# A two-block transformer kernel in which 96 instead of 64 tokens take the gathered expert path, 416 instead of 448 stay dense, and VectorE instead of GpSimd writes the low parts of the expert weights from the 53rd column on

## What is computed

```python
def peer_ffn(x, w_q, sub_keys, expert_u, expert_v):
    ...
    e = (jnp.take_along_axis(i1, ci // P_TOPK, axis=-1) * N_KEYS
         + jnp.take_along_axis(i2, ci % P_TOPK, axis=-1))
    g = jax.nn.softmax(vals, axis=-1)
    ...
        a = jnp.einsum('cd,ckd->ck', xc, expert_u[ec])
        w = (gc * jax.nn.gelu(a.astype(jnp.float32))).astype(x.dtype)
        return jnp.einsum('ck,ckd->cd', w, expert_v[ec])
```

## Time and profile before

| | us |
|---|---|
| median of three runs (lowest, highest) | 2789.0 (2784.4, 2793.2) |
| profiled execution, span | 2786.5 |
| TensorE busy | 2673.9 |
| VectorE busy | 1865.4 |
| GpSimd busy | 1708.2 |
| ScalarE busy | 907.8 |

### The profile page before, as it was taken

One profiled execution on the slowest core, in us unless ns is written; L12 is line 12 of the kernel. 1 busy time (PEld: TensorE's weight loads), 2 busy tenths in 40 slices (PEclk: granted clock), 3 DMA queues, 4 the chain that ended last, 5 costly groups with the idle time before them and its releaser, 6 DMA issues.

```text
span 2786.5 us, 36945 instructions
## 1 busy us (share of the span) xinstructions
PE 2673.9 (96%) x13184; PEld 2229.0 (80%) x13184; DVE 1865.4 (67%) x2466; ACT 907.8 (33%) x1531; POOL 1708.2 (61%) x755
## 2 busy tenths in 40 slices
PE   6999999999997999998999999999999999999999
PEld 4777778888874876445888888999998999999998
DVE  7999973372335525764549983999964677777777
ACT  2223222101123144663234343444432333333332
POOL 5888887878873611003745555777786566666665
PEclk9999999999998998999999999999999999999999
DMA  3443334423331321001325555888898676767764
GB/s 143 134 135 131 129 124 137 134 95 133 114 109 59 113 99 68 1 1 63 114 98 151 142 150 176 259 286 286 286 325 314 238 263 240 270 248 260 259 248 162
DMA packets 171121, 466.67 MB, mean 167 GB/s; under 512 B 12832, under 2 KB 86688, under 8 KB 171040
## 3 DMA queue, kind: packets, MB, share of 16 engines
q1 hardware_dynamic: 152608, 398.53, 43.2%
q0 software_dynamic: 18432, 67.12, 6.7%
HBM read 404.78 MB, written 60.82 MB: 167 GB/s over the span
## 4 chain that ended last, share of the span: by engine, by line
PE 80%; issue 7%; DVE 6%; POOL 4%; ACT 1%; DMA 1%; POOLq 0%; SPq 0%; DVEq 0%; ACTq 0%
PE ps L1016 37%; PE ps L553 30%; POOL spl L2091 3%; PE ps L951 2%; PE ps L1037 2%; PE ps L644 1%; PE ps L928 1%; PE ps L911 1%; PE ps L569 1%; DVE hnt L1490 1%; DVE hl L1494 1%; PE ps L907 1%; PE ps L870 1%; PE ps L739 1%; PE ps L816 1%
## 5 line engine op out<-in xcount | busy, mean ns | idle before, releaser
L2091 POOL TENSOR_TENSOR spl<-ring,spl 128x1024 fp32r<-128x1024 f32 x256 | 669.9, 2617 | 482.6 <-ACT spl L1368 482.4
L2024 POOL TENSOR_TENSOR spl<-ring,zero 128x1024 fp32r<-128x1024 f32 (+1 forms) x180 | 367.7, 2043 | 528.2 <-PE ps L553 459.9
L553 PE MATMUL ps<-hh,spl 128*128 128x512 f32 x2064 | 652.3, 395 | 20.3 <-DVE hl L1494 7.9
L1016 PE MATMUL ps<-wsp,spl 128*128 128x448 f32 x3072 | 626.7, 366 | 4.6 <-issue 4.6
L1016 PEld LDWEIGHTS ps<-wsp,spl 128*128 128x128 f32 x3072 | 578.3, 188 | 50.6 <-POOL spl L2091 5.0
L1016 PE MATMUL ps<-hh,spl 128*128 128x448 f32 x2048 | 601.4, 369 | 6.7 <-POOL spl L2091 6.7
L1368 ACT ACTIVATE spl<-ring 128x1024 fp32r<-128x1024 f32 x256 | 271.7, 1061 | 795.4 <-PE ps L1016 793.8
L2026 POOL TENSOR_TENSOR spl<-ring,spl 128x1024 fp32r<-128x1024 f32 (+1 forms) x180 | 479.5, 2664 | 14.1
L553 PEld LDWEIGHTS ps<-hh,spl 128*128 128x128 f32 x2064 | 389.9, 189 | 115.5 <-issue 15.4
L1982 DVE TENSOR_TENSOR wsp<-gl,wsp 128x448 fp32r<-128x448 f32 x128 | 315.3, 2464 | 167.6 <-ACT wsp L1413 167.3
L1016 PEld LDWEIGHTS ps<-hh,spl 128*128 128x128 f32 x2048 | 385.3, 188 | 42.4 <-issue 9.3
(11 more groups left out here) (341 smaller groups left out, 3291.1 us busy)
## 6 DMA issues: line engine op xcount, KB each, us to landing
ring<-stream_in SPq DMA_DIRECT2D x196, 704.0 KB, 4.1
ring<-u_in SPq DMA_DIRECT2D x128, 512.0 KB, 4.1
ring<-v_in SPq DMA_DIRECT2D x128, 512.0 KB, 3.5
gelu<-gst SPq DMA_DIRECT2D x128, 224.0 KB, 4.1
dense<-stage SPq DMA_DIRECT2D x14, 2048.0 KB, 13.9
gl<-gelu SPq DMA_DIRECT2D x32, 896.0 KB, 5.8
gw<-dense SPq DMA_DIRECT2D x32, 896.0 KB, 8.5
x<-x_in SPq DMA_DIRECT2D x4, 512.0 KB, 6.8
```

The costliest lines, as they stand in the source:

```text
L553: m = pe.matmul(ps[:, bank, :], w[:, part, k0 + k * n:k0 + k * n + P], rhs(k), start=first and k == 0 and part == 0 and rhs is high, stop= ...
L1016: m = pe.matmul(ps[:, bank, 0:TD], w[:, part, k0 + k * P:k0 + (k + 1) * P], rhs(k), start=first and k == 0 and part == 0 and rhs is high, ...
L2024: pool.tensor_tensor(w[:, 0, 0:n], ring[:, j, 0:n], zero[:, :].to_broadcast([P, n]), ALU.add).then_inc(wt_high, 1)
L2091: pool.tensor_tensor(spl[:, j % 2, 1, 0:D], ring[:, j, 0:D], spl[:, j % 2, 0, 0:D].bitcast(F32), ALU.subtract).then_inc(lo_done, 1)
```

## The change

96 tokens take the gathered path, in two blocks: the last 64 as before (two partition halves, 64 gathers), and the 32 before them four times (four partition quarters, 32 gathers), with rows, accumulator and fold matmuls of their own (`xt2`, `acc2`, `folds[1]`). 416 tokens stay dense: every dense matmul streams 416 columns, every save, gate load and `weigh` shrinks alike, and there are 13 slabs and not 14, so the one-hots, spreads and stores end four units earlier, after unit 103. The gathered rows of the v stage have six slots and not four. From unit 52 on VectorE writes the low parts (`weight_low`), placed by hand among its one-hots, dots, `low`, `weigh` and `add_row`; GpSimd then only issues gathers. 36 dots are spread in the one-hot loop (6 in 8 units, as before), two in the last slab, and the other 58 lie in the 23 units 105 to 127, two or three ahead of each unit's low part.

```diff
@@ -47,11 +47,15 @@
 GB = 16
 TB = 32
 QUAD = 4
-RARE = 64
+PICKS = E_H * E_K
+RARE_BLOCKS = [(64, 2), (32, 4)]
+RARE = sum(n for n, _ in RARE_BLOCKS)
 TD = T - RARE
 SLABS = TD // TB
-RARE_SLOTS = E_H * E_K // 2
-U_SLOTS, V_SLOTS = 6, 4
+RARE_AT = [0, PICKS // 2]
+RARE_SLOTS = sum(PICKS // k for _, k in RARE_BLOCKS)
+U_SLOTS, V_SLOTS = 6, 6
+SPREAD_DOTS = 6
...
+def rare_slot(s, i=0, per=0):
+
+    m, r = divmod(s, 3)
+    if r < 2:
+        return 0, i * (per // 3 * 2) + (RARE_AT[0] + 2 * m + r)
+    return 1, i * (per // 3) + (RARE_AT[1] + m)
...
-                        m = pe.matmul(bank[half * RARE:(half + 1) * RARE, :], rows[:, c, TD:T].bitcast(F32), cc("ident"),
+                        m = pe.matmul(bank[half * 64:(half + 1) * 64, :], rows[:, c, T - 64:T].bitcast(F32), cc("ident"),
+                                      start=rows is hh, stop=rows is hl)
+            for c in range(DC):
+                bank = ps[:, 6 + c // 4, c % 4 * P:(c % 4 + 1) * P]
+                for rows in (hh, hl):
+                    for part in range(4):
+                        m = pe.matmul(bank[part * 32:(part + 1) * 32, :], rows[:, c, TD:TD + 32].bitcast(F32), cc("ident"),
...
-                            pe.wait_ge(acc_done, RARE_SLOTS + 1)
-                        pe.matmul(ps[:, c % DC, TD:T], acc[:, c % DC * P:(c % DC + 1) * P], fold, start=True, stop=True)\
+                            pe.wait_ge(acc_done, RARE_SLOTS + 2)
+                        pe.matmul(ps[:, c % DC, TD:TD + 32], acc2[:, c % DC * P:(c % DC + 1) * P], folds[1], start=True, stop=True)
+                        pe.matmul(ps[:, c % DC, T - 64:T], acc[:, c % DC * P:(c % DC + 1) * P], folds[0], start=True, stop=True)\
                             .then_inc(y_part, 1)
...
+            def weight_low(at, i=None, per=0):
+
+                dve.wait_ge(hi_done, at + 1 if i is None else i * per + (at + 1))
+                dve.tensor_tensor(spl[:, at % 2, 1, 0:D], ring[:, at % RING, 0:D], spl[:, at % 2, 0, 0:D].bitcast(F32),
+                                  ALU.subtract).then_inc(lo_done, 1)
+
+            def dot(s, i=None):
+
+                row = s % U_SLOTS
+                dve.wait_ge(u_row[row], 16 * (s // U_SLOTS + 1) if i is None else i * 16 + 16)
+                block, at = rare_slot(s, i if i is not None else 0, SPREAD_DOTS)
+                dve.scalar_tensor_tensor(out=rows_of[row], in0=rows_of[row], scalar=1.0, in1=xts[block], op0=ALU.mult, op1=ALU.mult,
+                                         accum_out=dots[:, one_at(at)]).then_inc(dot_done, 1)
+
+            dve.wait_ge(lo_done, RING + U_PLAIN)
+            weight_low(U_PLAIN)
...
+            with dve.Fori(0, SLABS // 2) as b:
+                    one_hots(j, b, bass.ds(b * (4 * GB) + j * GB, GB))
+                    weight_low(U_PLAIN + 2 * j + 1, b, 8)
+                    for s in range(j * SPREAD_DOTS // 4, (j + 1) * SPREAD_DOTS // 4):
+                        dot(s, b)
+                    weight_low(U_PLAIN + 2 * j + 2, b, 8)
+            s, last = SLABS // 2 * SPREAD_DOTS, U_PLAIN + 4 * SLABS
+            for j in range(2):
+                at = SLABS // 2 * 4 * GB + j * GB
+                one_hots(j, SLABS // 2, slice(at, at + GB))
+                weight_low(last - 4 + 2 * j + 1)
+                dot(s)
+                s += 1
+                weight_low(last - 4 + 2 * j + 2)
+            first, left = last + 1, RARE_SLOTS - s
+            for e in range(first, N_KEYS):
+                for _ in range(left * (e - first + 1) // (N_KEYS - first) - left * (e - first) // (N_KEYS - first)):
+                    dot(s)
+                    s += 1
+                weight_low(e)
+            dve.wait_ge(oh_ready, 2 * SLABS)
...
+            def unit_pair(i, p, to_weigh=None):
+
+                for k in (2 * p, 2 * p + 1):
+                    weight_low(N_KEYS + k, i, 16)
+                    low(i, k)
+                if to_weigh is not None:
+                    weigh(*to_weigh)
+                for s in range(p * 12 // 8, (p + 1) * 12 // 8):
+                    add_row(i, s)
...
-            u_at, v_at = 0, 0
-            for n in range(U_PLAIN, 2 * N_KEYS):
-                column(n // RING, n % RING)
-                while u_at < RARE_SLOTS and u_unit_of(u_at) <= n:
-                    u_gather(u_at)
-                    u_at += 1
-                while u_at == RARE_SLOTS and v_at < RARE_SLOTS and N_KEYS + 2 * v_at - 3 <= n:
-                    v_gather(v_at)
-                    v_at += 1
+            for s in range(RARE_SLOTS):
+                u_gather(s)
+            for s in range(RARE_SLOTS):
+                v_gather(s)
```

More of the change, by code:

```diff
@@ L505, in _ @@
                             store(i, k)
+            for j in range(RING):
+                u_load(U_PLAIN // 4 + 1 + SLABS, j)
+                save_late(U_PLAIN // 4 + 1 + SLABS, j)
+                if j == 1:
+                    store(SLABS // 2, 0)
             for i in range(U_PLAIN // 4 + 2 + SLABS, N_KEYS // 4):
@@ L1072, in _ @@
                     spread(i, 2 * k + 1)
+            for k in range(4):
+                u_unit(U_PLAIN // 4 + SLABS - 1, k)
+                spread(SLABS // 2, 2 * k)
+                spread(SLABS // 2, 2 * k + 1)
             with pe.Fori(U_PLAIN // 4 + SLABS, N_KEYS // 4) as i:
@@ L1430, in _ @@
                     evacuate(i, 2 * k + 1)
+            for k in range(4):
+                gelu_unit(U_PLAIN // 4 + SLABS - 1, k)
+                evacuate(SLABS // 2, 2 * k)
+                evacuate(SLABS // 2, 2 * k + 1)
             with eng.Fori(U_PLAIN // 4 + SLABS, N_KEYS // 4 - 1) as i:
@@ L1928, in _, with late @@
-            for half in range(2):
-                dve.tensor_copy(share[half * RARE:(half + 1) * RARE, :],
-                                sel[P - RARE:, TT - 1, 2, half * RARE_SLOTS:(half + 1) * RARE_SLOTS]).then_inc(share_ready, 1)
-            step(dve.tensor_tensor(fold, cst[:, CST["ident"][0]:CST["ident"][0] + RARE],
-                                   cst[:, CST["ident"][0] + RARE:CST["ident"][1]], ALU.add))
-            def dot(s, row, ready):
-                dve.wait_ge(u_row[row], ready)
-                dve.scalar_tensor_tensor(out=u_rows[row], in0=u_rows[row], scalar=1.0, in1=xt, op0=ALU.mult, op1=ALU.mult,
-                                         accum_out=dots[:, s]).then_inc(dot_done, 1)
+            def late(block, part, k):
+                n, parts = RARE_BLOCKS[block]
+                first = TD % P + sum(m for m, _ in RARE_BLOCKS[block + 1:])
+                return sel[first:first + n, TT - 1, k, part * PICKS // parts:(part + 1) * PICKS // parts]
@@ new lines, in picks_of @@
+            def picks_of(tile, block, part):
+                n, parts = RARE_BLOCKS[block]
+                return tile[part * n:(part + 1) * n, RARE_AT[block]:RARE_AT[block] + PICKS // parts]
+            parts_of = [(block, part) for block in range(2) for part in range(RARE_BLOCKS[block][1])]
+            for block, part in parts_of:
+                dve.scalar_tensor_tensor(out=picks_of(place, block, part), in0=late(block, part, 1), scalar=float(N_KEYS),
+                                         in1=late(block, part, 0), op0=ALU.mult, op1=ALU.add).then_inc(place_ready, 1)
```

110 lines of the change are left out of this document (50 added, 60 removed).

## The result

The changed kernel takes 2706.7 us (median of 4 runs, 2701.3 to 2708.8); the kernel before took 2786.7 us beside it (4 runs, 2782.5 to 2793.2). The ratio is 0.9708, with a 95% interval of 0.9682 to 0.9733: 2.9% faster. The profiled execution took 2706.1 us with a span of 2704.2. All medians and ratios leave out slow executions, that is one, among the six of the kernel with the first low parts ahead of the gelu, at 7632 us.

What follows compares the result with a forecast made beforehand. The prediction took the number of matmuls by the distance between them, plus few waits, as the bound. Savings of 75.2 us less 24 and 6 us of new waits gave 45 us off 2786.5: 2742 us, range 2715 to 2775.

Steps and rivals of the forecast that it cites:

- rows turned: Before unit 0, more tokens turned into rows: 128 more matmul records, taken as a cost of 5.5 us.
- the new waits: TensorE waiting behind VectorE's low parts between units 105 and 130, as transfers saturate: 15 to 45 us.
- The last 23 u units and the turn: Units 105 to 127 move 49.8 MB at 359 GB/s, 24 us of waits; 6 us more at the v stage's start.
- The transfers keep up: Rival: gathers and loads run at 400 GB/s or more, waits under 12 us, time 2720 to 2728 us; chance 0.17.
- The v stage: 128 units of 24 matmuls, each 13.3 ns shorter with 416 columns: 40.9 us saved.
- Units 0 to 51: Early u units: 16.6 us saved by shorter matmuls, less grown waits for GpSimd's low parts, leaving 11.2 us.
- The first one-hots: At the first spread, TensorE's 5.5 us wait for VectorE's first one-hots falls by 2.0 us.
- the slab less: One slab fewer leaves 4 units without spreads: 3.6 us saved.
- units 52 to 104: Middle u units, with shorter matmuls and low parts hidden on VectorE: 19.9 us saved.
- VectorE's order is too tight: Rival: v stage misses its 0.5 us or spread stretch stays at 281 GB/s; 2752 to 2778 us; chance 0.17.
- gathers one at a time: Rival: in the last u units each gather must land before the next moves; about 2987 us, at least 2831; chance 0.05.
- 416 columns are no faster: Rival: another limit holds matmuls at about 200 ns, so 82 us do not come; about 2810 us; chance 0.04.

Runs made afterwards that it cites:

- mixed passes: The 448-column kernel with VectorE low parts and the changed kernel, each v-stage pass multiplying four different widths; one execution each, 2766.4 and 2691.5 us.

## Why the prediction was wrong

**The mechanism was right, a rate was wrong.** Every term of the sum but the rows turned shows with its sign, the low parts on VectorE are hidden in the spread stretch (5.51 us a unit, forecast 5.50) and in the v stage, and the new waits stood where they were put, from unit 105 on, with a share over 1.0: 11.0 us behind VectorE's low parts, and 4.1 behind ScalarE. Four sizes were off, all to the same side.

**The last 23 u units and the turn: 15.8 us of the 37.** This is the step that failed, "At 359 GB/s ... it takes 139 us". The measured rate is 411 GB/s over units 105 to 126, and 418 in the stretch inside. The row of 359 GB/s was hardly one "of loads and gathers". Its packets, from 2040 to 2050 us in the kernel before, and then those of the changed kernel from 2015 to 2110 us:

```profile
DMA packets 4562, 3.59 MB, mean 359 GB/s; under 512 B 64, under 2 KB 4227, under 8 KB 4562
```

```profile
DMA packets 12377, 39.71 MB, mean 418 GB/s; under 512 B 1375, under 2 KB 3992, under 8 KB 12375
```

93% of the packets of the first are under 2 KB, most of them of the slab's store that SyncE had issued at 2035.9 us (2 MB in pieces of 512 bytes, 128 numbers in `QUAD * TB`), and only 0.87 of its 3.59 MB are gathers. In the second it is 32%. Full stretches beside such a store moved 359, 341 and 311 GB/s (shares 1.07, 1.06 and 1.02), full ones without it 406, 411 and 418 (1.02, 1.03 and 1.03). No run changed the size of the packets alone, so that they set the rate is read from these stretches, not tested. My 49.8 MB over 418 GB/s are 119 us, 14.6 more than the 104.5 that TensorE needs; units 105 to 126 took 114.1 - 99.4 = 14.7 us more than the same units without waits. Of these 11.0 are waits and 1.6 a lower clock behind one of them. The 4 MB that I let lag would have brought it to 5.

That is 10.3 us of the 15.8; the other 5.6 are the turn. I had put 6 us there; the piece of units 127 and 128 takes 16.6 us against 16.8 before, and 14.9 when there is no backlog. The transfers are behind there, but before the change about as much was lost for another reason (4.6 us between the stages), and the two do not add up.

None of the rivals fits as written. *The transfers keep up* had the right condition (400 GB/s or more) and a chance of only 0.17. But the transfers did not keep up: the waits of 15.1 us are over its 12 and at the lower end of the forecast's own 15 to 45, and the time is under its 2720 to 2728, since the other terms were off to the same side. For the rate, a page spoke for it: the Trainium skill (DMA: Bandwidth & Descriptors, "Where 436 GB/s comes from") gives the 435 GB/s, and the 418 over 95 us come near it. The same section also says that transfers between HBM and SBUF are bound at about 358 GB/s a core. The trace does not agree: nearly all of the 411 and 418 GB/s are such transfers. Of small packets the page ("Why small descriptors are slow") says that each costs about three cycles whatever its size. That agrees in kind with the lower rate beside the slab's store. By an estimate from the page's count a piece of 512 bytes loses 3 cycles in 19, some 16%; no run here tests that figure.

**The v stage: 7.2 us.** "The bounds are 12.9 and 14.2" ns for 32 columns. In the profiled execution it was 202.7 - 186.7 = 16.0 ns (564.48 us for 126 units of 24). In five other executions with 416 columns and VectorE's low parts the same units take 569.5 to 572.3 us (the longest with 2.3 us of waits), 188.3 ns, and there it is 14.4. The matmuls from 2190 to 2620 us, without a wait, in the changed kernel and in the one with eight dots a pass:

```profile
2190.00:2620.00 430.00, 430.00 (x2306) 429.33 (x2305) 1.00 0.81 300
```

```profile
2190.00:2620.00 430.00, 430.00 (x2285) 427.45 (x2284) 1.00 0.80 298
```

The kernel with the first low parts ahead of the gelu has the faster pace too (x2305). The runs with other widths show why bounds by lines from 280 and 512 columns could not hold: the extra over the columns changes with the width, and 448 has more of it than both ends. The term was mis-sized by 3 us or by 8, depending on the pace. Only one execution of each variant was profiled, so what decides between the two stays open.

**Units 0 to 51: 7.4 us.** Of TensorE's busy time 258.3 - 238.8 = 19.5 us went, 15.6 ns a matmul instead of 13.3: 2.9 us of the miss. The rest are the waits. I let them grow by 3.9 us (each of 12 by 0.32) and 1.5 more; they grew from 6.0 to 6.9. Without the long one of 2.2 us before, which has no successor, eleven waits went from 0.35 us on average (3.8 / 11) to 0.63 (6.9 / 11), so the 0.3 us each were right. The base was not: two other executions with 448 columns and the same code in these units waited 2.4 us (ten times) and 3.2 (eleven times) over the same stretch. From there to 6.9 it is 3.7 to 4.5, near what I added, so most of this part of the miss seems to be that the profiled execution before waited longer than others do.

**Rows turned: 5.8 us.** I put 128 records at 57 ns, 7.3 us, or half of it, and took 5.5. Four column quarters do overlap more than two halves: 128 records in 3.6 us, 28 ns each. The rest is not explained by the change; the start of unit 0 differs by up to 9 us between executions.

**What held.** The first one-hots 3.8 us (3.5 forecast); the slab less and units 52 to 104 within 1 us; VectorE's low parts 1224 ns and dots 1220 ns beside GpSimd's gathers; no waits in the v stage, where by my estimate half a microsecond was all there was to spare. Of the other rivals, *VectorE's order is too tight* is refuted by the profile after (no waits in the v stage, 297 GB/s in the spread stretch), by the run with every other gather left out, and even more by the one with 128 tokens; *gathers one at a time* and *416 columns are no faster* by the profile after.

## What to carry to other kernels

Before a rate is taken from a saturated stretch, look at which packets it moved, and over how long: the same engines were full at 359 GB/s over 10 us beside a store in small pieces, and at 411 to 418 over 95 us and more without it. Take the rate where the share is at 1 and not by dividing: the quotient of rate and share was 399 in units 105 to 126 and 345 with every other gather left out. Test the halves of a change apart and together: one alone gave 0.2%, the other nothing, both 2.9%, because the freed time of one was taken back by the engine that the other relieves. And where a transfer-bound stretch shows one big stall behind one big transfer, move bytes out of the stretch (13 us) before splitting the transfer (nothing).

## What the runs showed of the hardware that was not expected

- Gathers of 64 rows into partitions 0 to 63 fill the DMA engines at 271 GB/s, where those of 128 rows reach 411 in the same place, and a 512 KB load beside them lands in 19.0 us instead of 7.4 (6.0 with every other gather left out). The Trainium skill (SBUF — State Buffer, "Door 1: The DMA port swizzle (why `[64,N]` ≈ `[32,N]`)") says that partitions 0 to 63 reach 8 of the 16 ports, 218 GB/s at most. The trace agrees with the direction, since into alternating halves the rate was 292; but the share was 1.04 there too, so it is not all.
- The extra of a matmul over its columns is not one figure: 13.3 ns at 400 columns, 15.0 at 408, 16.7 at 440 and 19.6 at 448 in mixed passes, 16.0 at 448 among its own kind. And 416 columns have two paces, 186.7 ns (two executions) and 188.3 (five), that an execution keeps through the v stage.
- TensorE came back from a wait of 4.1 us at the 1.2 GHz level: the granted clock was 0.53 over the 3.5 us that followed, and ten matmuls took 1.6 us longer than at full clock. The row:

```profile
2023.78:2027.25 3.47, 3.47 (x10) 3.32 (x11) 0.53 1.03 415
```
